# Shared-expert products of a mixture-of-experts step moved to later expert pairs, a fixed third pair, and another order of the last returns

## The reference

```python
def _moe(h, w_router, router_bias, we_g, we_u, we_d, ws_g, ws_u, ws_d):
    ...
    w = w / jnp.sum(w, axis=-1, keepdims=True) * ROUTED_SCALE
    combine = jnp.einsum('tk,tke->te', w, jax.nn.one_hot(idx, N_EXPERTS, dtype=jnp.float32)).astype(h.dtype)
    hid = jax.nn.silu(jnp.einsum('td,edf->tef', t, we_g)) * jnp.einsum('td,edf->tef', t, we_u)
    routed = jnp.einsum('tef,efd->td', hid * combine[..., None], we_d)
    shared = (jax.nn.silu(t @ ws_g) * (t @ ws_u)) @ ws_d
    return (routed + shared).reshape(b, length, d)
```

## Time and profile before

| | us |
|---|---|
| median of 3 runs | 894.68 |
| lowest and highest | 894.6, 896.19 |
| the profiled execution | 893.01 |
| its span (first to last instruction) | 891.2 |
| its granted TensorE clock | 0.996 of full speed |

### The profile page before, as it was taken

The page is one execution under the profiler, slowest core; times in us unless marked ns, Lnnn a source line. Parts: engine busy times, 40 slices in busy tenths (PEclk is TensorE's granted clock), DMA queues, the critical chain, the costliest instruction groups (busy, mean ns, idle before and its releaser), DMA issues.

```text
span 891.2 us, 11381 instructions
## 1 busy us (share of the span) xinstructions
PE 867.7 (97%) x4186; PEld 445.8 (50%) x4186; DVE 472.3 (53%) x1030; ACT 166.8 (19%) x349; POOL 58.2 (7%) x75
## 2 busy tenths in 40 slices
PE   8999999999999999999999999999999999999894
PEld 6774446776655547654444444444444444434332
DVE  4645398936796945524354344544535354544447
ACT  4131012020000034121111211212111111212113
POOL 1020100000000000200000000000000000000000
PEclk9999999999999999999999999999999999999998
DMA  9999433512575847499999999999999999999992
GB/s 328 389 367 234 146 127 126 198 48 94 216 279 203 348 204 260 152 384 419 417 412 419 419 419 419 413 416 414 418 420 419 420 420 419 421 418 419 417 377 87
DMA packets 63626, 288.00 MB, mean 323 GB/s; under 512 B 6472, under 2 KB 6528, under 8 KB 38480
## 3 DMA queue, kind: packets, MB, share of 16 engines
q1 hardware_dynamic: 56176, 265.60, 75.3%
q0 software_dynamic: 7392, 21.63, 6.5%
HBM read 287.34 MB, written 4.33 MB: 327 GB/s over the span
## 4 chain that ended last, share of the span: by engine, by line
PE 89%; DMA 7%; DVE 2%; SPq 1%; issue 1%; ACT 0%; DVEq 0%
PE bank L1252 24%; PE bank L830 12%; PE bank L1277 11%; PE bank L823 9%; PE bank L1293 9%; DMA ring<-in_w_exp_up 5%; PE bank L1047 5%; DMA ring<-in_w_ada 2%; PE bank L1094 2%; PE bank L1194 2%; PE bank L1197 1%; PE bank L835 1%; PE bank L840 1%; PE bank L1291 1%; PE bank L1002 1%; PE bank L1000 1%
## 5 line engine op out<-in xcount | busy, mean ns | idle before, releaser
L1252 PE MATMUL bank<-ring,QK 128*64 128x512 f32 (+1 forms) x1056 | 226.6, 595 | 4.5 <-DMA ring<-in_w_exp_up 4.5
L2259 DVE TENSOR_TENSOR hT<-bank,hT 128x512 f32<-128x512 f32 x174 | 109.7, 685 | 82.7 <-PE bank L1293 81.8
L1252 PEld LDWEIGHTS bank<-ring,QK 128*64 128x64 f32 (+1 forms) x1056 | 70.5, 128 | 126.2 <-issue 126.2
L2248 DVE SCALAR_TENSOR_TENSOR VG<-VG,cw,bank 128x256 f32<-128x256 f32 x32 | 15.4, 481 | 169.1 <-issue 163.1
L1277 PE MATMUL bank<-ring,VG 128*64 128x512 f32 (+1 forms) x512 | 102.2, 598 | 0.6 <-ACT MB L1585 0.6
L830 PE MATMUL bank<-hT,ring 128*128 128x384 f32 x256 | 86.0, 489 | 0.0
L823 PE MATMUL bank<-ring,hT 128*128 128x512 f32 x192 | 82.7, 593 | 0.0
L1293 PE MATMUL bank<-y_hi,slotT 128*128 128x512 f32 x180 | 80.9, 450 | 0.0
L1293 PE MATMUL bank<-y_lo,slotT 128*128 128x512 f32 x180 | 71.1, 395 | 0.0
L1639 ACT CAST y_hi<-bank 128x512 fp32r<-128x512 f32 x60 | 32.4, 591 | 194.9 <-PE bank L1293 191.7
L830 PEld LDWEIGHTS bank<-hT,ring 128*128 128x128 f32 x256 | 47.8, 190 | 33.7 <-issue 2.4
(11 more groups left out here) (405 smaller groups left out, 951.8 us busy)
## 6 DMA issues: line engine op xcount, KB each, us to landing
ring<-in_w_exp_gate SPq DMA_DIRECT2D x56, 1024.0 KB, 11.0
ring<-in_w_exp_up SPq DMA_DIRECT2D x56, 1024.0 KB, 13.6
ring<-in_w_exp_down SPq DMA_DIRECT2D x56, 1024.0 KB, 15.5
ring<-in_w_ada SPq DMA_DIRECT2D x12, 2048.0 KB, 12.0
ring<-in_w_in SPq DMA_DIRECT2D x9, 2048.0 KB, 18.0
spare<-in_w_exp_gate SPq DMA_DIRECT2D x8, 1024.0 KB, 10.1
spare<-in_w_exp_up SPq DMA_DIRECT2D x8, 1024.0 KB, 12.8
spare<-in_w_exp_down SPq DMA_DIRECT2D x8, 1024.0 KB, 16.0
```

Source lines behind the costliest of these rows:

```text
L1252: ins = mm(ps[0][rows, :], xT[:, k, rows], gate_up_of(p, n)[:, k, :, :], start=(k == 0), stop=(k == KC - 1))
L2259: v.tensor_tensor(into, o, into, ALU.add).then_inc(sem("summed"), 1)
```

## The change

It has four parts.

1. **Shared products later.** `sg2` leaves the place behind `gate_up(0)` and is made behind `gate_up(4)` (`third_gate`), its turn `shT2` behind `gate_up(5)` (`third_T`). The twelve shared down products are added to the returned tiles of pairs 3 to 14 where they were added to those of pairs 0 to 11 (`SHARED_FROM`). Buffers move with it: the third tile of the turned tokens lies in `MB`, `y_hi` and `y_lo` lie in `S0` and `work`, DVE keeps `su2` in a buffer of its own with one more copy.
2. **A fixed third pair.** `AHEAD` holds six experts where it held four. SP takes experts 8 and 9 for pair 2 without reading `tab_order`, and waits for `order_ready` only before pair 3. The load of the second half of the shared down weights waits for an earlier tile (`h2T11`).
3. **Returns of pair 30.** Three of its six tiles are returned before `hidden_T(31)`, three behind it.
4. **Returns of pair 31.** For each half the three `y_hi` matmuls are issued as soon as `y_hi` is there, then the three `y_lo` matmuls. On DVE the first `y_lo` half is made before the second half is weighed.

The core of the diff:

```diff
@@ -33,13 +33,15 @@
 NEXT = LAST % 2
-AHEAD = (4, 5, 6, 7)
+AHEAD = (4, 5, 6, 7, 8, 9)
 UNEVEN = 5
...
 FURTHER = 44
+THIRD_AT = 4
+SHARED_FROM = 3
 EPS = 1e-6
@@ -196,7 +198,7 @@
     out.extend([("su1", "S", 7), ("su2", "S", 1), ("order", "V", 2), ("tokens0a", "A", 4), ("tokens0b", "A", 5)])
-    out.extend([("sg2", "G", 7), ("shT0", "A", 2), ("shT1", "A", 3), ("rounds", "V", 2), ("shT2", "A", 3)])
+    out.extend([("shT0", "A", 2), ("shT1", "A", 3), ("rounds", "V", 2)])
     return out
@@ -588,9 +592,13 @@
             sp.dma_start(x0_rows, x[:, 0, :]).then_inc(sem("x0_parked"), 16)
-            sp.wait_ge(sem("order_ready"), 1)
             for p in range(2, PAIRS):
-                e = [sp.value_load(column(tab_order, 2 * p + n), min_val=0, max_val=E - 1) for n in range(2)]
+                if p == 3:
+                    sp.wait_ge(sem("order_ready"), 1)
+                if 2 * p < len(AHEAD):
+                    e = AHEAD[2 * p:2 * p + 2]
+                else:
+                    e = [sp.value_load(column(tab_order, 2 * p + n), min_val=0, max_val=E - 1) for n in range(2)]
                 for n in range(2):
...
                 if p == 2:
-                    computed(sp, "shT2")
+                    computed(sp, "h2T11")
                     sp.dma_start(sd_w[1], w_sd[:, 1, :]).then_inc(sem("shared_in"), 16)
@@ -1091,16 +1099,30 @@
                 for k in range(lo, hi):
-                    ins = mm(o[:, 0:ED], hT[:, k, t * P:(t + 1) * P], w[:, k, :], start=(k == 0), stop=(k == KC - 1))
+                    ins = mm(o[:, 0:ED], h2T[t][:, k, :], w[:, k, :], start=(k == 0), stop=(k == KC - 1))
                 if hi == KC:
...
                 emptied(pe, f"su{t}")
-                o = bank(f"shT{t}")
+                done(shared_T_in(bank(f"shT{t}"), t))
+            def shared_T_in(o, t):
                 for j in range(2):
                     ins = nc.tensor.transpose(o[:, j * P:(j + 1) * P], s_hid[t][:, j:ED:2], ident)
-                done(ins)
+                return ins
+            def third_gate(p):
+                pe.wait_ge(sem("summed"), 6 * (p - 2) + 5)
+                for k in range(KC):
+                    ins = mm(ps[7][:, 0:ED], h2T[2][:, k, :], sg_w[:, k, :], start=(k == 0), stop=(k == KC - 1))
+                ins.then_inc(sem("third_done"), 1)
+            def third_T(p):
+                pe.wait_ge(sem("third_ready"), 2)
+                pe.wait_ge(sem("summed"), 6 * (p - 2) + 5)
+                shared_T_in(ps[7], 2).then_inc(sem("third_done"), 1)
@@ -1281,14 +1303,16 @@
                 o, k = ps[banks[g]][:, :], p % KEEP
-                shared = p < 2 * 6 and g == p // 2
+                n, j = divmod(p - SHARED_FROM, 2)
+                shared = n == g
                 if shared:
-                    j = p % 2
-                    if p == 0:
-                        emptied(pe, "shT2")
-                    if p == 1:
+                    if g == 0 and j == 0:
+                        emptied(pe, "shT1")
+                    if g == 0 and j == 1:
                         pe.wait_ge(sem("shared_in"), 64)
-                    mm(o, shT_sb[:, t, j, :], sd_w[j][:, h * 512:(h + 1) * 512], start=True, stop=False)
+                    if g == 4:
+                        pe.wait_ge(sem("third_ready"), 3)
+                    mm(o, shT_sb[t][:, j, :], sd_w[j][:, h * 512:(h + 1) * 512], start=True, stop=False)
                 for n, y in enumerate((y_hi, y_lo)):
@@ -1343,38 +1367,54 @@
                         pe.wait_ge(sem("xT_ready"), 2 * (p + 2) + g - 2)
+                    if g == 0 and p + 1 in (THIRD_AT, THIRD_AT + 1):
+                        pe.wait_ge(sem("third_ready"), 1 if p + 1 == THIRD_AT else 3)
                     if g == 3:
...
-            def scatter_two(p):
-                first = p == LAST - 2
-                if first:
+            def return_part(p, n, y, start, stop):
+                t, h = LAST_TILES[n]
+                return mm(ps[LAST_BANKS[n]][:, :], slotT[p % KEEP][:, t * P:(t + 1) * P], y[:, h * 512:(h + 1) * 512], start=start, stop=stop)
+            def scatter_next_to_last(tiles):
+                p = LAST - 2
+                if 0 in tiles:
                     pe.wait_ge(sem("summed"), 6 * p)
-                for n, (t, h) in enumerate(LAST_TILES):
-                    if n == 0 or not first and n == 3:
-                        pe.wait_ge(sem("lo_ready"), 2 * p + (2 if first or n else 1))
-                    if first and LAST_BANKS[n] == 1:
+                    pe.wait_ge(sem("lo_ready"), 2 * p + 2)
+                for n in tiles:
+                    if LAST_BANKS[n] == 1:
                         pe.wait_ge(sem("hidT_ready"), LAST)
-                    o = ps[LAST_BANKS[n]][:, :]
-                    for i, y in enumerate((y_hi, y_lo)):
-                        ins = mm(o, slotT[p % KEEP][:, t * P:(t + 1) * P], y[:, h * 512:(h + 1) * 512], start=(first and i == 0), stop=(not first and i == 1))
-                    ins.then_inc(sem("scattered"), 1)
+                    return_part(p, n, y_hi, True, False)
+                    return_part(p, n, y_lo, False, False).then_inc(sem("scattered"), 1)
+            def scatter_last():
+                p = LAST - 1
+                for h in range(2):
+                    tiles = range(3 * h, 3 * h + 3)
+                    pe.wait_ge(sem("hi_ready"), 2 * p + h + 1)
+                    for n in tiles:
+                        return_part(p, n, y_hi, False, False)
+                    pe.wait_ge(sem("lo_ready"), 2 * p + h + 1)
+                    for n in tiles:
+                        return_part(p, n, y_lo, False, True).then_inc(sem("scattered"), 1)
...
             gate_up(0)
-            shared_hidden("sg", sg_w, 2)
             tokens_of(1)
...
             count_rounds()
-            shared_T(2)
             down(0)
...
                 gate_up(p)
+                if p == THIRD_AT:
+                    third_gate(p)
+                if p == THIRD_AT + 1:
+                    third_T(p)
                 tokens_of(p + 1)
...
             gate_up(LAST - 1)
+            scatter_next_to_last(range(3))
             hidden_T(LAST - 1)
-            scatter_two(LAST - 2)
+            scatter_next_to_last(range(3, 6))
             down(LAST - 1)
-            scatter_two(LAST - 1)
+            scatter_last()
...
                 pe.wait_ge(sem("hid_ready"), p)
-                stand_alone(pe, "pe_passed")
+                stand_alone(pe, "passed")
                 gate_up_duo()
...
                 pe.wait_ge(sem("down_next"), q * 32 + 32)
-                stand_alone(pe, "pe_passed")
+                stand_alone(pe, "passed")
                 down_duo()
...
                 pe.wait_ge(sem("summed"), p * 6)
-                stand_alone(pe, "pe_passed")
+                stand_alone(pe, "passed")
                 for g in range(6):
@@ -1652,16 +1693,18 @@
                 silu(p)
-                if p == 0:
-                    shared_silu(2)
+                if p == THIRD_AT:
+                    act.wait_ge(sem("third_done"), 1)
+                    nc.scalar.activation(s_silu, ps[7][:, 0:ED], ACT.Silu).then_inc(sem("third_ready"), 1)
+                if p == THIRD_AT + 1:
+                    act.wait_ge(sem("third_done"), 2)
+                    nc.scalar.copy(shT_sb[2], ps[7][:, 0:ED].rearrange("p (j t) -> p j t", j=2)).then_inc(sem("third_ready"), 1)
                 if p < LAST - 1:
...
                 hidden_T(p)
-                if p == 0:
-                    shared_T(2)
                 if p in slot_gate:
@@ -2203,6 +2246,7 @@
             shared_hidden(1)
+            v.tensor_copy(s_hid[2], tile("su2")[:, 0:ED]).then_inc(sem("emptied_S"), 1)
@@ -2267,16 +2311,25 @@
                 dve.wait_ge(sem("gates_in"), 16 * (j + 1))
-                for h in range(2):
+                def gated(h):
                     cut = slice(h * 512, (h + 1) * 512)
...
                     v.tensor_tensor(y_gated[h], ps[2 + h][:, :], slot_gate[p][:, cut], ALU.mult).then_inc(sem("y_gated"), 1)
-                for h in range(2):
+                def low(h):
                     cut = slice(h * 512, (h + 1) * 512)
...
                     v.tensor_tensor(y_lo[:, cut], y_gated[h], y_hi[:, cut], ALU.subtract).then_inc(sem("lo_ready"), 1)
+                gated(0)
+                if j:
+                    low(0)
+                gated(1)
+                if not j:
+                    low(0)
+                low(1)
@@ -2335,8 +2389,8 @@
                 if p == 0:
-                    shared_hidden(2)
                     count_rounds()
+                    dve.wait_ge(sem("table_ready"), 1)
                     remainder(p)
...
                     picks(n, k, slotT[k], ps[6][:, 0:T], 6 if n < PAIRS - UNEVEN else 14)
+                if p == THIRD_AT:
+                    dve.wait_ge(sem("third_ready"), 1)
+                    v.tensor_tensor(s_hid[2], s_silu, s_hid[2], ALU.mult).then_inc(sem("third_ready"), 1)
```

54 lines of the change are left out of this document (29 added, 25 removed).

## The result

The changed kernel took 898.12 us (median of 10 runs) against 895.37 for the kernel before on the same chip (median of 10): ratio 1.0029, 95% interval [1.0019, 1.0039]. A second comparison gave 1.0017 [1.0002, 1.0032]. The forecast was 0.8 us faster; the time lies above its range. The profiled execution shown here is 899.22 us, span 897.4, against 893.01 and 891.2 before.

What follows compares the result with a forecast made beforehand. The stream of weights was taken to hold the end. The terms -0.78 (closed hole) + 0 + 0 gave -0.8 us, so 894.68 - 0.8 = 893.9 us, with a range from 891.2 to 896.0.

Steps and rivals of the forecast that it cites:

- D: Rival: unit 6's early load delays POOL's third row write, gate_up(0) ends 2.1 us later, 896.0 us; chance 0.10.
- I take the write as hidden: Third row write beside unit 6's load: half the rate turns its 2.9 us into some 4.5, at no cost.
- its threshold: In D, before gate_up(0): a third row write landing in up to 6.6 us costs nothing; 8.7 us is 3.2 late.
- the term of -0.8: Sum of the parts, -0.78 + 0 + 0, taken from the median of 894.68 us.
- The hole in the stream: Weight stream at 397.5 us: moving shared products out of pair 0 issues unit 10 earlier and closes it, -0.78 us.
- The same work comes back later: Pairs 4, 5 and behind pair 11: the moved shared products are hidden by the weight stream's backlog, 0.
- Unit 6 earlier is worth 0 to the stream: Pair 2's load comes 18 us earlier, but unit 7 still waits for the end of gate_up(0): 0, bounds 0 and -0.35.
- The 2 us from issue to first bytes: Weight loads of units 6, 7 and 10: first bytes were taken to flow 2 us behind the issue.
- The two waits at the end: PE's waits of 1.2 and 1.4 us in the last returns: filling them gives 0, bounds +0.35 and -2.6.

Runs made afterwards that it cites:

- a_half: Changed kernel with only unit 6's first gate matrix (1 MB) loaded early, the rest behind the row and weights' writes: 894.34 us, 0.9986 of the kernel before.
- after_again: The changed kernel unaltered, measured a second time: 896.46 us, 1.0017 of the kernel before.
- a_first: Changed kernel with SP issuing unit 6 only when the banks of the third h2 tile are emptied: 897.82 us (one run).
- b_end: Kernel before with only the new returns of the last two pairs and DVE's new order of weighing and y_lo: 896.23 us, ratio 1.0002.
- a_act: Changed kernel with the third row write and the weights' columns write issued by ScalarE on its hardware queue: 896.57 us, 1.0011 of the kernel before.
- a_wait_rows: Changed kernel with unit 6 loaded only when the three h2 row writes have landed: 898.22 us, 1.0032 of the kernel before.
- a_sp: Changed kernel with the third row write issued by SP on its own queue right ahead of unit 6's load: 895.46 us, 1.0001 of the kernel before.
- a_sort6: Changed kernel with four experts named ahead and unit 6 behind the sort again: 893.71 us, 0.9984 of the kernel before.
- b_shared: Kernel before with only the shared products moved (third gate in pair 4, down products from pair 3): 894.70 us, ratio 0.9996.
- b_unit6: Kernel before with only experts 8 and 9 named ahead, so unit 6 loads without waiting for the sort: 897.87 us, ratio 1.0033.
- a_sort6_again: Second measurement of the changed kernel with unit 6 behind the sort: 894.50 us, 0.9994 of the kernel before.
- a_warm: Changed kernel with unit 6 behind the sort, plus seven unread matmuls before the last two gate/up products: 901.80 us, 1.0080 of the kernel before.

## Why the prediction was wrong

**The step that failed** is in "The rivals", D: "I take the write as hidden: half of the rate turns its 2.9 us into some 4.5." The write beside the load took 7.47, 8.81, 9.06 and 9.23 us in the four profiles that issue the 2 MB at once and the write from POOL. The mechanism of D and its chain were right, and its threshold nearly: `gate_up(0)` is late by the landing less 6.2 us in each: 7.07 gives +0.87 (a_half), 7.47 +1.28, 8.81 +2.62, 9.06 +2.87, and 9.23 +3.04 beside 1.69 of half clock (after_again). I had put the threshold at 6.6 and the size at 2.1 for a landing of 8.7, and nothing of it into the sum. With 9.06, 6.2 and the term of -0.8, the sum would have been 894.68 + 2.9 - 0.8 = 896.8. The measured 898.12 is 1.3 us more: 0.7 is the kernel before itself, whose median is 895.37 over ten runs and not 894.68. The remaining 0.6 is less than one stretch of half clock costs, and isn't explained further.

The reason why I took 4.5 was the rate. I let two transfers share the engines from the start, each slowed to half, while the traces show that what was issued ahead of the write goes first for the most part: one packet of the write in four microseconds of the changed kernel's profile, until 1.6 of 2.1 MB had passed. Only then do they share. A row that should have stopped me stood in the sum's own group: two of three row writes of before, those among weight loads, took 6.1 and 8.7 us. I took the smallest of three rows, the one with nothing beside it, for a write that would have 2 MB beside it; a cost that the trace shows only under the other condition should be taken from the rows of that condition. D at 0.10 was too small for the same reason.

The Trainium skill ("DMA: Bandwidth & Descriptors", section on queues, rings and completion order) says that an engine drains a whole packet of some 9 to 17 descriptors, at most 64, from one row before it goes to the next. I had quoted the rule as "a packet at a time" and read its packets as the 8 KB packets of the profile. If each of the profile's packets is one of its descriptors, which nothing here shows, the rule speaks for D: a matrix of 1 MB is 8 of the profile's packets on each of 16 engines, so one or both matrices can pass before the write has its turn. That would agree with the 1 packet in four microseconds and with a_half. The stretch of a_first from 363 to 366 us, 105 packets of the load and 100 of the write, looks more like turns of one of the profile's packets each; the profile doesn't name the engine of a packet, so what holds the write's first packets back stays **open**.

**The hole in the stream**: right. Expected -0.78 us; from `gate_up(0)` to `gate_up(31)` the profiles without the moved products take 490.04, 490.50 and 490.55 us, those with them and with unit 6 behind the sort 488.68 to 489.92 (mean of five 489.16): -1.2 us, and the two groups don't overlap. With unit 6 early they take 489.19 to 489.73 where `gate_up(0)` ran at full clock.

**The same work comes back later** at no cost: right, by the same numbers, and PE's waits for weights (5.0 us) were there to cover it.

**Unit 6 earlier is worth 0 to the stream**: right; unit 7 left 7.06 us after `gate_up(0)` began, when that had ended. It was issued at 356.02, later than my 354.3 by the shift of this run. The 2 us from issue to first bytes were read from slices that are too coarse: unit 6's first packet of before is between 373.0 and 373.5 us, some 1 us behind its issue, and SP's queue moves packets again from 398.5, 1.5 us behind the issue of unit 10. That leaves the sum as it is.

**The two waits at the end** are worth 0: right. The last `y_lo` began 18.0 us behind the start of `gate_up(31)` (1.69 of it the clock), the first addition followed its end by the same 0.51 us, and b_end measures 1.0002.

**Clock**: not in the sum at all. In four of the nine profiles with an early unit 6 PE ran at half clock behind its pause of 2.0 to 2.8 us between 367 and 375 us, in none of the eight others. In a_act and after_again it stood at 0.50 for 3.4 us, at a cost of 1.7 us; in a_wait_rows and a_sp, where PE waited for the first gather, for 6.8 us, at some 2.8 us. The changed kernel itself had it once (behind 2.80 us) and once not (behind 2.63). That adds to D's cost in part of the runs. In ten of seventeen profiles a like stretch stands between 846 and 872 us. In `gate_up(30)` it is nearly free, since PE then waits less for the last weights: in a_sort6 `gate_up(30)` takes 8.77 us and PE waits 0.53 us ahead of `gate_up(31)`, where the other two profiles of that kernel, at full clock, have 2.64 and 1.66. In `gate_up(31)` it costs 1.7, and there I saw it in both profiles of the changed kernel, in b_end and in a_act, all four with the new order of the end. Whether that order makes it more frequent is **open**: b_end's time doesn't show it, and the mean granted clock of all its runs, 0.9936, is that of b_shared beside it (0.9935), which has the old order.

## What to carry to other kernels

A transfer that is moved early into an idle stretch isn't free if a small one that others wait for is issued within it: look not at the average traffic but at what is issued in the next microseconds, and count the small transfer as landing when the large one does (here within a microsecond of unit 6's last matrix, in the changed kernel, b_unit6 and a_first). Issue the small one first, or hold the large one until the last small one has landed; a wait on only the first of several just moves the collision to the next. And where a row exists under the same condition as the planned one, price with that row, even if a quieter one fits the argument better.

## What was new about the hardware

- A 512 KB write that is issued with or up to 2.4 us behind 2 MB of loads on another queue lands in 7.5 to 9.2 us, alone in 2.9 to 3.1; on ScalarE's hardware queue it is the same 9.1, and ahead of the load on the load's own queue 3.0. A write of 96 KB went from 2.2 or 2.3 to 4.1 to 6.9 us, a gather from 4.7 to 7.2.
- Most of the load issued ahead of such a write passes before the write's packets begin (1.3 to 1.75 of 2.1 MB, 0.9 of 1.05); what comes after shares packet for packet (35 and 35 in one microsecond of a_first), at 395 GB/s together.
- The granted clock fell to 0.50 for 3.4 us, twice for 6.8, after pauses of PE of 2.0 us and more, and not after each of them: PE waited 2.48 us ahead of two products in a_half and 2.64 us in a_sort6_again, and all ran at full clock.
- The returns' products of 128x512 stand 0.23 us apart in PE's timeline; a product of the same size of the gathered rows with themselves (a_warm) ran as two passes of 0.44 us.
